# A three-layer transformer kernel: value projections by token block first, a fourth high-part buffer, modulation slices turned by fours

## The reference, cut to what matters

```python
def first_block(x, c, ctx, c_ctx, ...):
    s_lat, s_ctx = silu(c), silu(c_ctx)
    for i in range(2):
        ml = split(s_lat @ w_ada[i] + b_ada[i], 6)     # modulation: 6*1024 values, latent
        mc = split(s_ctx @ w_ada[i] + b_ada[i], 6)     # and context
        u_lat, u_ctx = modulate(h_lat, g_pre_mix[i], ml[0], ml[1]), modulate(h_ctx, ..., mc[0], mc[1])
        o = even_mixer(...) if i % 2 == 0 else odd_mixer(...)
        h_lat = h_lat + ml[2] * rms_norm(o_lat, g_post_mix[i])
        f = sqrelu_mlp(modulate(h_lat, g_pre_ff[i], ml[3], ml[4]), w_ff1[i], w_ff2[i])
        h_lat = h_lat + ml[5] * rms_norm(f, g_post_ff[i])
        ...                                            # the same for h_ctx in layer 0
def odd_mixer(u_ctx, u_lat, w_in, ...):
    p = u @ w_in        # qC kC vC (512 each), qD (512), kD vD (128 each)
    c_lat = neighbourhood_attention(...)               # with a bias table c_rpb
    d_lat = global_block_attention(axial_rope(rms_norm(qD)), axial_rope(rms_norm(kD)), vD, ...)
def second_block(x, ...):
    h = rms_norm(x); proj = h @ w_in                   # NSA q, kv, gates; retention q, k, v, gate; merge gates
    ...                                                # NSA attention, retention, merge, gated convolution ffn
```

## Time and profile before

| | |
|---|---|
| median of three runs | 2058.32 us (2055.95 to 2064.08) |
| profiled execution, its own time | 2063.38 us |
| its span | 2061.6 us |
| PE busy | 1844.8 us (89%) |
| DVE, ACT, POOL busy | 1100.0, 904.6, 216.2 us |

### The profile page before, as it was taken

One profiled execution on the slowest core, in us unless ns is written; L12 is line 12 of the kernel. 1 busy time (PEld: TensorE's weight loads), 2 busy tenths in 40 slices (PEclk: granted clock), 3 DMA queues, 4 the chain that ended last, 5 costly groups with the idle time before them and its releaser, 6 DMA issues.

```text
span 2061.6 us, 39782 instructions
## 1 busy us (share of the span) xinstructions
PE 1844.8 (89%) x16802; PEld 1537.0 (75%) x16802; DVE 1100.0 (53%) x1671; ACT 904.6 (44%) x1448; POOL 216.2 (10%) x214
## 2 busy tenths in 40 slices
PE   5899879899888889999996999799979999679997
PEld 3777658778777778888886776698877677569985
DVE  1457565465555554324435766565445674556863
ACT  3326545344332353223325356565342465346652
POOL 0000034425253000000000200010000000000210
PEclk9999889999998989999998999899989999789998
DMA  8332233222231222333233420355544434245543
GB/s 272 94 123 90 91 112 105 85 84 84 84 105 64 82 82 82 102 102 93 91 102 72 124 81 28 107 182 187 192 131 155 152 103 139 72 132 164 184 156 110
DMA packets 201375, 237.16 MB, mean 115 GB/s; under 512 B 14347, under 2 KB 158573, under 8 KB 201197
## 3 DMA queue, kind: packets, MB, share of 16 engines
q1 hardware_dynamic: 195856, 227.33, 34.7%
q10 hardware_dynamic: 5341, 7.30, 1.0%
HBM read 233.56 MB, written 1.05 MB: 114 GB/s over the span
## 4 chain that ended last, share of the span: by engine, by line
PE 75%; DVE 11%; ACT 7%; issue 2%; POOL 2%; DMA 1%; SPq 1%; ACTq 1%; DVEq 0%; POOLq 0%
PE bank L1412 18%; PE bank L1413 17%; PE bank L1414 17%; PE bank L1604 9%; ACT window L2473 2%; DVE window L1906 2%; PE bank L1592 2%; PE bank L1571 2%; PE bank L1583 2%; PE bank L1463 1%; PE bank L1611 1%; SPq L2934 1%; PE bank L1789 1%; ACT arena L2538 1%; PE bank L1575 1%
## 5 line engine op out<-in xcount | busy, mean ns | idle before, releaser
L1412 PE MATMUL bank<-window 128*128 128x512 f32 (+1 forms) x2152 | 768.6, 357 | 64.8 <-DVE window L1955 27.8
L1413 PE MATMUL bank<-window 128*128 128x512 f32 (+1 forms) x2152 | 754.1, 350 | 0.0
L1414 PE MATMUL bank<-window 128*128 128x512 f32 (+1 forms) x2152 | 753.8, 350 | 0.0
L1412 PEld LDWEIGHTS bank<-window 128*128 128x128 f32 x2152 | 419.6, 195 | 131.1 <-DVE window L1906 32.4
L1906 DVE TENSOR_TENSOR window<-arena,window 128x2048 fp32r<-128x2048 f32 (+1 forms) x164 | 371.4, 2265 | 272.3 <-ACT window L2473 270.4
L2473 ACT ACTIVATE window<-arena 128x2048 fp32r<-128x2048 f32 (+3 forms) x292 | 377.1, 1291 | 198.3 <-PE bank L1414 121.4
L1414 PEld LDWEIGHTS bank<-window 128*128 128x128 f32 x2152 | 419.0, 195 | 50.9
L1413 PEld LDWEIGHTS bank<-window 128*128 128x128 f32 x2152 | 420.2, 195 | 48.1 <-issue 0.2
L2473 ACT ACTIVATE arena<-bank 128x256 f32<-128x256 f32 (+1 forms) x298 | 127.0, 426 | 370.7 <-PE bank L1414 134.9
L1604 PE MATMUL bank<-arena 64*64 64x64 f32 (+1 forms) x5888 | 218.1, 230 | 18.9 <-DVE arena L1398 10.5
L1604 PEld LDWEIGHTS bank<-arena 64*64 64x64 f32 x5888 | 204.8, 139 | 35.4 <-DVE arena L1398 12.2
(11 more groups left out here) (286 smaller groups left out, 1668.1 us busy)
## 6 DMA issues: line engine op xcount, KB each, us to landing
arena<-in_w_ff SPq DMA_DIRECT2D x64, 1024.0 KB, 5.3
arena<-in_w_ada SPq DMA_DIRECT2D x48, 1024.0 KB, 5.7
arena<-in_w_in SPq DMA_DIRECT2D x23, 1024.0 KB, 5.1
arena<-in_w_ffn_up SPq DMA_DIRECT2D x22, 1024.0 KB, 5.1
arena<-in_w_ffn_down SPq DMA_DIRECT2D x10, 1024.0 KB, 5.1
arena<-in_w_in_even SPq DMA_DIRECT2D x9, 1024.0 KB, 5.5
arena<-in_w_out SPq DMA_DIRECT2D x8, 1024.0 KB, 5.1
arena<-in_w_in_odd SPq DMA_DIRECT2D x8, 1024.0 KB, 5.3
```

The lines of the kernel that those rows point to most:

```text
L1412: e.matmul(o, rr(l[0]), rr(r[0]), start=start, stop=False)
L1413: e.matmul(o, rr(l[0]), rr(r[1]), start=False, stop=False)
L1414: return e.matmul(o, rr(l[1]), rr(r[0]), start=False, stop=stop)
```

## The change

- **Modulation by fours.** Four slices sum into one bank: SV grows from 32 to 38 columns, and slice g of a four takes it shifted by 6 - 2g, so that its two rows (latent, context) land two rows further down in each row group. Then come one ACT copy, one turn with a selector of 8 columns in place of 2, and one DVE addition of 16 columns. The bank is held over the four.
- **A fourth HIGH buffer**, `extra[:, 0:2048]`, joins the turn (`lend`) from the end of the recurrence to the odd start, from the end of the odd attention to `r_proj`, and from the end of the second attention on. `back` takes it out.
- **`early` becomes a list.** Halfway through the blocks of an `out_proj` with `then` (m = ntok/2 - 1) a second place is noted. The split of the second chunk to come behind that `out_proj` goes there.
- **Odd layer.** The last `out_proj` of ff0 gets `ahead=local_values`: before out block 3 it takes the four vC banks, loads both vC chunks, and projects the first half of token block 0. Then come the rest of vC by token block with block 3's trail behind the first, then qD, kD, vD, with bias loads behind each projection, then "odd start". `c_proj` keeps one bias load, qC and kC. The projections of vC wait for their own token block, not for all.
- **Second block.** `out_proj` no longer trails by itself. vr 0 is projected by token block first, with the trail behind its first half; then qN and kv; "second start" follows. `r_proj` starts at vr 1.

```diff
-    early = [None]
+    HIGH.append(extra[:, 0:2048])
+    ring_free, high_free = [()] * len(RING), [()] * 4
+    turns = [0, 1, 2]
+    early = []
...
+    def lend(name):
+        high_free[3] = tuple(stage(name))
+        turns.insert(1, 3)
+    def back():
+        turns.remove(3)
...
-                i = high_at[0] % 3
-                high_at[0] += 1
+                i = turns.pop(0)
+                turns.append(i)
...
-            if early[0] is None:
+            if not early:
                 step("split", key)
             else:
-                plan.insert(early[0], ("split", key))
-        here()
+                plan.insert(early.pop(0), ("split", key))
+                early[:] = [n + 1 for n in early]
+        if not early or whole and len(early) == 1:
+            here()
...
     def mod(i, s):
         cols(("mod", i, s), I["w_ada"][i], s * 256, 256, whole=True)
-        take("mod", i, s)
+        if s % 4 == 0:
+            take("mod", i, s // 4)
         step("mod", i, s)
-        give("mod", i, s)
+        if s % 4 == 3:
+            order_of_turn.append((i, s // 4))
+            step("rows", i, s // 4)
+            give("mod", i, s // 4)
...
+                        if ahead and m == ntok - 1:
+                            ahead()
                         step("out block", name, c, m)
...
+                            if m == ntok // 2 - 1:
+                                early.append(len(plan))
...
         trailing[:] = then[-1:]
-        if ntok == 2:
-            trail()
...
+    def local_values():
+        for k in range(4):
+            take("vC", k)
+        for y in range(2):
+            cols(("vC", y), W_o, 1024, 512, y * 4, 4)
+        step("vC", 0, 0)
...
-    step("odd start")
+    for k in range(4):
+        if k:
+            step("vC", 0, k)
+        if k == 1:
+            trail()
+        step("vC", 1, k)
+        give("vC", k)
+    bias_loads = iter(range(0, len(bias_pairs), 4))
     for j in range(4):
         ...
         step("qD", j)
         give("qD", j)
-        if j > 1:
-            trail(2 * j - 3)
+        step("load bias", next(bias_loads))
...
+    step("odd start")
+    back()
...
     def c_proj():
-        for k in range(4):
-            take("vC", k)
-        for y in range(2):
-            cols(("vC", y), W_o, 1024, 512, y * 4, 4)
-            for k in range(4):
-                step("vC", y, k)
-                ...
-                step("load bias", next(bias_loads))
-                yield
+        step("load bias", next(bias_loads))
...
-    step("second start")
+    def values_gates(nm, j, c0, between=lambda: None):
+        for k in range(2):
+            take(nm, j, k)
+        for y in range(2):
+            cols((nm, j, y), W_2, c0 + j * 512, 512, y * 4, 4)
+        for k in range(2):
+            for y in range(2):
+                step("vg", nm, j, y, k)
+                if not k and not y:
+                    between()
+            give(nm, j, k)
+    values_gates("vr", 0, 2328, trail)
...
+    step("second start")
...
-            for j in range(n):
+            for j in range(nm == "vr", n):
...
         # PE
+                t = e.matmul(u.b[q:q + 32, 0:256], SV[:, k, 6 - 2 * g:38 - 2 * g], w.v[:, k, :], start=g == 0 and k < 4, stop=g == 3 and k >= 4)
...
-                t = e.matmul(u.b[:, 2 * f:2 * f + 2], a[:, f * 128:f * 128 + 128], sel, start=True, stop=True)
+                t = e.matmul(u.b[:, 8 * f:8 * f + 8], a[:, f * 128:f * 128 + 128], sel, start=True, stop=True)
```

More of the change, by code:

```diff
@@ L917, in program @@
     ring_free[2:NSLOT] = [tuple(stage("units"))] * 2
-    high_free[:] = [tuple(stage("units"))] * 3
+    high_free[0:3] = [tuple(stage("units"))] * 3
     here()
@@ L934, in program @@
     O_e = sb(4, 1024)
+    lend("recurrence")
     gains(0, "g_pre_ff", 4, 1)
@@ L990, in ffn @@
             out_proj(("ff2", i, part), parts, F.h1, ntok, F.O, (), {j: [at("ff1 part", i, part, j)] for j in range(nt)},
-                     part > 0, end, then=[normed(T, k, True) for k in range(ntok)] if end else ())
+                     part > 0, end, then=[normed(T, k, True) for k in range(ntok)] if end else (), ahead=ahead if end else None)
         return x_ready(T, range(ntok))
-    xr = ffn(0, 4, xr, "m1", lambda f, s: DER[:, 2, f, s:s + 1], lambda f, s: MOD[1][:, f, s:s + 1], [*stage("mix0")])
+    W_o, odd_x = I["w_in_odd"][0], x_ready("m1", range(4))
+    def local_values():
[4 more added lines that the diff above has]
+        step("vC", 0, 0)
+    ffn(0, 4, xr, "m1", lambda f, s: DER[:, 2, f, s:s + 1], lambda f, s: MOD[1][:, f, s:s + 1], [*stage("mix0")], local_values)
     norms["m1"].made = [at("gain", 2)]
@@ L1029, in program @@
     give("kD")
+    step("load bias", next(bias_loads))
     cols(("vD",), W_o, 2176, 128)
-    take("vD", 0)
-    step("vD", 0)
-    give("vD", 0)
-    take("vD", 1)
-    step("vD", 1)
-    give("vD", 1)
+    for part in range(2):
+        take("vD", part)
+        step("vD", part)
+        give("vD", part)
+        step("load bias", next(bias_loads))
+    step("odd start")
+    back()
     c_done = []
-    bias_loads = iter(range(0, len(bias_pairs), 4))
     def c_proj():
-        for k in range(4):
-            take("vC", k)
-        for y in range(2):
-            cols(("vC", y), W_o, 1024, 512, y * 4, 4)
-            for k in range(4):
-                step("vC", y, k)
-                if y:
-                    give("vC", k)
-                step("load bias", next(bias_loads))
-                yield
+        step("load bias", next(bias_loads))
         for j in range(4):
@@ L1119, in program @@
     OP_o = Pair(sb_aligned(8, 256), OT_o)
+    lend("odd attention")
     step("gate", 1, 2)
@@ L1256, in r_proj @@
                         rotate((which, i), x, 256, Rr, cosr, sinr, tmpr, [at("ret consts"), at("qkr", "kr", 3)])
+    back()
     run(n_prepare(), r_proj())
     step("end", "second attention")
+    lend("second attention")
     top[0] = m_n
@@ L1458, in mod @@
         def mod(i, s):
-            w, u = chunks["mod", i, s], bank("mod", i, s)
+            w, u, g = chunks["mod", i, s], bank("mod", i, s // 4), s % 4
             pe.wait_ge(w.landed, u.before, at("sv"))
@@ L1770, in qN_ @@
         def qN_(j):
-            fm(chunks["qN", j // 2], (j % 2) * 128, X, N256, bank("qN", j), *second_x, last=j % 2)
+            fm(chunks["qN", j // 2], (j % 2) * 128, X, N256, bank("qN", j), last=j % 2)
         def kv_(nm, g):
@@ L2841, in final @@
             e.activation(tiny[:, 4 * k + 1:4 * k + 2], a, ACT.Sqrt, scale=1.0 / 1024, bias=eps).then_inc(*sc.tick(at("final root", k)))
-        steps = {"load h": load_h, "more columns": more_columns, "silu": silu, "mod": mod, "split": split, "spread": spread,
+        steps = {"load h": load_h, "more columns": more_columns, "silu": silu, "rows": rows_, "split": split, "spread": spread,
                  "square": square, "root table": root_table, "scale rows": scale_rows, "x": norm_x, "x hi": x_hi,
```

95 lines of the change are left out of this document (47 added, 48 removed).

## The result

Twenty runs of each kernel: 2065.81 us after (2061.65 to 2075.42), 2063.18 us before (2055.95 to 2068.40), ratio 1.0024 with a 95% interval of 1.0014 to 1.0034. That is 5 us more (0.0024 x 2063), where 11.6 less was forecast. It lies within 0.5%, and outside the range of 2032 to 2062. The profiled execution took 2068.36 us, its span is 2066.6.

What follows compares the result with a forecast made beforehand. PE, busy 89% of the span, was taken as the bound, with its waits and low clock. Terms -14.2 - 1 + 3.7 - 5.5 + 8 - 2.6 = -11.6 took the median from 2058.32 to 2047 us, range 2032 to 2062.

Steps and rivals of the forecast that it cites:

- The odd layer's filler: Head norms and D attention: eight vC rounds no longer run beside them; +8 us, bounds +3 and +13.
- The turns: Modulation: 48 turns become 12, each worth 0.53 us of PE; -14.2 us in sum, held bank's 1 us included.
- The held bank: Recurrence: one bank held over four slices leaves seven to rotate; 1 us of a possible 0 to 4 counted against.
- ff0 to the odd layer: Joint behind ff0, new order with vC pieces between norm links: 19.4 us lost against 25; -5.5, bounds 0 and -10.
- mix1 to ff1: Joint before ff1: the split, hidden before, now stands in the norm's chain; +3.7 us, bounds 0 and +4.5.
- ff1 to the second block: Joint behind ff1: early split, vr (0,0) fills a wait, DMA issues behind kv; -2.6 us, bounds 0 and -6.
- mix0 to ff0: Joint before ff0: the norm's chain is later, the wait for the split goes; -1 us, bounds 0 and -3.5.
- Fourth buffer: Fourth high buffer in the steady feed-forward, where PE idles 0.33 us of 342: 0 gain.
- Rival 2: Joints eat the gain: splits on all four chains, odd +10, turns -14 or less; about 2055 us, chance 0.21.

Runs made afterwards that it cites:

- x1: The changed kernel measured once more, unaltered; ratio 1.0030 to the kernel before.
- x3: The kernel before with the two matmuls of every modulation turn issued twice; ratio 1.0074 to the kernel before.
- x4: The kernel before with one bank withheld for the whole recurrence; ratio 0.9998 to the kernel before.
- e3: The changed kernel without the second early split place where there are two token blocks (layer 1); ratio 1.0006 to the kernel before.
- y4: The same kernel as e8, measured again; median 2044.91 us, ratio 0.9930 to the kernel before.
- e8: The kernel before with only the modulation by fours and the second block's new order; median 2048.38 us, ratio 0.9945 to the kernel before.
- e4: The changed kernel with no second early split place at all, the rest kept; ratio 1.0017 to the kernel before.
- e5: The changed kernel with the last two head norms given own buffers and started two rounds earlier; ratio 1.0047 to the kernel before.
- e2: The changed kernel with the odd layer put back as before; ratio 0.9982 to the kernel before.
- e6: The changed kernel with the eight bias loads back at the rounds of c_proj; ratio 1.0059 to the kernel before.
- x2: The changed kernel with GpSimd's mask addition waiting for the last head norm; ratio 1.0058 to the kernel before.
- y2: The kernel before with GpSimd's mask addition shrunk to 16 columns of one head; ratio 0.9999 to the kernel before.

## Why the prediction was wrong

- **The odd layer's filler, +8 in the prediction: right in kind, wrong in size, and this decides.** The three waits were named rightly (squares, last two norms, the attention's start). They were priced at 2, 2.6 and 3 and measured 3.5 (2.38 and 1.11), 4.95 and 3.3 (2.65 and 0.62); two waits that were not named added 2.1 (0.89 and 1.20), and the slower clock 3.6 in place of 2. The step that failed is the price of the norms and of the attention's start, "end about 2.6 after the last kC" and "some 3 until its own pipeline is full", together with the clock behind them: they were taken as if the eight rounds left would go as far into the chain as before. They don't, because the four qC rounds now lie where vC lay. The term measured +15.6 in the first profile, over the stated bound of +13, and 22.6 in x1, where GpSimd's addition met a split. That meeting was in the trace of before, beside the vC rounds; the prediction looked at GpSimd only for the bias.
- **The turns, -14.2: right in kind, over by 4.** Measured -9 to -11. The failed step is the factor: 0.53 us of PE for a turn was nearly right (x3: 0.45), but only 0.32 of it reaches the time, where the busy shares 0.97 and 0.91 were taken for that. The wider selector cost next to nothing, as said (256 ns median of a record in the changed kernel, 251 before). The even stage gave 0.2 in the profile, where 3.1 was counted because PE was busy 97% of it.
- **The held bank:** 1 counted, 0 measured (x4, -3 to +2).
- **ff0 to the odd layer, -5.5:** -6.6. The hand-made schedule held: waits of 3.29, 3.36, 0.76 and 6.19 in place of 3.1, 3.9, 0.6 and 9.1. The last is the one that was over-priced, by 3.
- **mix1 to ff1, +3.7:** +3.8, and e3 takes it away. **ff1 to the second block, -2.6:** -1.8, in which the early split costs: without it -4.4 to -5.2 (y4, e8). **mix0 to ff0, -1:** +0.5 in the profiles; the wait for the split went as forecast, and the norm's wait grew from 2.1 to 6.5. **Fourth buffer, 0:** no run took it out alone; e4, which keeps it, shows no gain from it.
- **The sum:** the terms measured are -10 + 0.5 - 6.6 + 15.6 + 3.8 - 1.8 = +1.5, with 0 to 7 for the meeting, against +5 measured. What stays open is how these 7 us share out over executions.
- **Rival 2**, that the joints eat the gain, came nearest to the outcome, by luck. Its own terms (-14, +4.5, +10) add up to +0.5 and not to "between 0 and -6", and with turns of -10 to +4.5. But three of four joints did about as forecast, and the loss lay behind them, in the stage that lent its filler.

## What to carry to other kernels

Work that is moved out of a stage to fill a gap elsewhere is taken from whatever it covered there. Before counting the gap filled, write down the longest chain of the stage it leaves and the PE work that is left beside it, round by round, not as a sum. In this kernel an early split gained at none of the four joints, because the engines that make it also carry the chain that PE is waiting for. And the time that an instruction takes of PE was more than removing it gave: doubling it in place measures both, the occupancy in the trace and the price in the median.

## What the runs showed of the hardware

A DVE split (two inputs, 128x2048) that starts while a GpSimd addition of 4.6 us is in progress ends 2.2 us behind the end of that addition, and the next addition then takes 6.5 to 6.7 us: 6.61 us for a split that takes 2.29 in x1, 4.36 in e5, 2.74 in the first profile, 5.98 before. Three norms that take 1.79 took 6.1 and 8.0 (e2, e6), and two operations of the rotation, 0.42 each, 3.64 and 4.60 (x2). The reciprocals, 6.93 us for 1024 columns, were never longer, beside GpSimd or not. Where the operation is hidden the median shows nothing (y2); where it lies on the chain the odd stage is 7 us longer in a profile (x1), and most of that is PE's work at a lower granted clock.

The profiles also differ by some 5 us before the odd layer for one and the same order: mix0's products ended at 720.6 and 716.2 in two profiles of the changed kernel, and at 727.5 and 722.0 in the kernel before and in y2. That is as much as the whole result, and why single profiles were read here by stage.
